# A two-layer decoder trunk: activations and norm weights laid out on the host, and another warm-up of TensorE

## The chip, the cores and the metric

The kernel runs on one core of one Trainium2 chip. The metric is the device time of one execution in microseconds (us); lower is better. TensorE (PE in the profile) multiplies, ScalarE (ACT) and VectorE (DVE) prepare its operands, GpSimd (POOL) does small things, and SyncE (SP) issues most of the loads. SP, ACT and POOL each have a DMA queue of their own; all queues share the core's 16 DMA engines.

## The reference, cut to what matters

Two layers work on 256 tokens of width 1024. What the change touches is the start of each layer, and the per-layer embedding `p`:

```python
h = x                                               # (256, 1024) float32
for i in range(DEPTH):                              # 2 layers
    f = swiglu(rms_norm(h, ffn1_pre_g[i]), ffn1_w_gu[i], ffn1_w_down[i])   # 1024 -> 2 x 2816 -> 1024
    h = h + 0.5 * rms_norm(f, ffn1_post_g[i])
    ...                                             # two attentions, merged by gates; a second SwiGLU
    gate = jax.nn.sigmoid(rms_norm(h, ple_pre_g[i]) @ w_ple_gate[i])
    e = (p[i] @ w_ple_proj[i]) * gate               # p[i]: (256, 256)
    h = h + rms_norm(e, ple_post_g[i])
```

All inputs are float32.

## The kernel before, in words

**Units and slots.** All weights are streamed once. They are cut into units of 1 MB (2048 columns on 128 partitions), numbered in the order in which TensorE uses them, and a unit lives in one of three slots (`SLOTS = 3`, unit number modulo 3) of three buffers: `raw` as loaded, `w_hi` and `w_lo` as split. Each product is made exact enough by three products of rounded parts: weight high x input high, weight low x input high, weight high x input low. So each unit is loaded by SP, its high part is rounded off by ACT (`high`, `high_piece`), its low part is subtracted by DVE (`low`, `low_piece`), and only then is it multiplied. The norm's weight vector (`ffn1_pre_g` and its like) is multiplied into the weights in these two steps (`scale=g_layer[...]`), so it must stand as a column over the partitions; the norm's root goes in behind the product, where the Silu reads it (`r_pre`). Products on TensorE wait for DVE's count `split_done` or `piece_split`.

**The head of the program.** Unit 0 is `w_ple_proj` (the product `p @ w_ple_proj` of layer 0 is made first and kept in `e_keep`); units 1 and 2 are the first 256 + 256 gate and up columns of layer 0's first SwiGLU (two halves of the 1024 input rows), unit 3 and unit 4 the next such columns, unit 5 the first rows of the down weights. Units 0 to 3 (`PIECED = 4`) are loaded, rounded and split in four pieces each, so that work can begin with the first quarter. Unit 3 uses unit 0's slot: SP issues its loads only when DVE has split all of unit 0. TensorE starts on unit 3 only when all four pieces are split (`begin`), and the second half of its columns only when the products of gate and up of units 1 and 2 are made for both token tiles (`prod_done`): that needs ACT's mean square of `h` (`square_pre`), POOL's root of it, ACT's Silu and DVE's product, for tile 0 and then for tile 1.

**ACT's order in the head** is written out by hand: pieces of units 0 to 2 between the inputs, two pieces of unit 3, `square_pre` of tile 0, the other two pieces of unit 3, the Silu of tile 0, `square_pre` of tile 1, half of unit 4, the Silu of tile 1, the other half of unit 4. Engines work through their instructions in this order; nothing overtakes.

**Turning.** TensorE needs the inputs with tokens last (input channels on the partitions), but `x` and `p` come with tokens on the partitions. So TensorE transposes them 128 x 128 at a time against an identity, into PSUM: `x` in four groups of four (`turn`), `p` in groups of two in layer 0 and one group of four in layer 1 (`turn_p`); ACT rounds the high part out of PSUM and DVE subtracts the low part. `x` is loaded into `h` (it is the residual too) in four loads of 256 KB on ACT's queue. The norm weights are loaded as rows by POOL and turned the same way in two steps (`turn_first_gain`, `turn_gains`). Until the first `p` is there, TensorE transposes the identity 13 and 3 times (`WARM_UP = (13, 3)`), so as not to stand idle.

Of the kernel before, what the change touches and what calls it, by code (L numbers as in the profile page):

```python
# [62 lines left out]
WARM_UP = (13, 3)  # L63
# [14 lines left out]
def trunk_kernel(nc, a, out):  # L78
    with ExitStack() as ctx:
# [34 lines left out]
        g_cols = sb("g_cols", [P, 4, (DEPTH + 1) * KD])  # L114
# [64 lines left out]
        p_nat = soft[:, :, 0:PLE]  # L179
# [9 lines left out]
        g_rows = mixed_t[:, P:2 * P]  # L189
# [21 lines left out]
        p_turned = sem("p_turned")  # L211
# [5 lines left out]
        h_loaded = [sem(f"h_loaded{n}") for n in range(2 * TT)]  # L217
# [56 lines left out]
        first_g = sem("first_g")  # L274
# [10 lines left out]
        p_in = [sem(f"p_in{t}") for t in range(TT)]  # L285
        first_g_in = sem("first_g_in")
# [5 lines left out]
        cols_turned = sem("cols_turned")  # L292
# [8 lines left out]
        blank = sem("blank")  # L301
        out_done = sem("out_done")
# [4 lines left out]
        HT_BANK, P_BANK, FIRST_P_BANK = 6, 7, (3, 5)  # L307
# [10 lines left out]
        GAIN_BANK = (4, 5)  # L318
# [48 lines left out]
        X_FIRST = (0, 2, 1, 3)  # L367
        X_FIRST_BANK = (0, 0, 1, 1)

        def p_bank(i, t=0):  # L370
            return bank(P_BANK if i else FIRST_P_BANK[t]).rearrange("p (k n) -> p k n", k=2)

        def nth_p(i, t):

            return i + 1 + (t if i == 0 else 1)

        def x_bank(i, q, idx):

            return bank((X_FIRST_BANK if (i, q) == (0, 0) else X_BANK[q])[idx])

        def nth_x(i, q, idx):

            return 20 * i + 4 * q + (X_FIRST.index(idx) if (i, q) == (0, 0) else idx) + 1

# [23 lines left out]
        def _(sp_):  # L408
            def load_p(t):
                sp_.dma_start(p_nat[:, t, :], a["p"][0, 0, t * P:(t + 1) * P, :]).then_inc(p_in[t], 16)  # L410

            for t in range(TT):
                load_p(t)
# [48 lines left out]
            for u in range(1, PIECED):  # L462
                load_pieces(u)
# [28 lines left out]
        def _(pool):  # L492
            pool.memset(ident[:, :], 0.0).then_inc(blank, 1)
# [3 lines left out]
            pool.dma_start(g_rows[0:2 * KD, :], a["ffn1_pre_g"].rearrange("l (k p) -> (l k) p", p=P)  # L497
                           ).then_inc(first_g_in, 16)
            for n, name in ((1, "mix_pre_g"), (2, "ffn2_pre_g"), (3, "ple_pre_g")):
                pool.dma_start(g_rows[2 * KD * n:2 * KD * (n + 1), :],  # L500
                               a[name].rearrange("l (k p) -> (l k) p", p=P)).then_inc(g_in, 16)
# [1615 lines left out]
```

## Time and profile before

| | us |
|---|---|
| three timed executions | 1174.38, 1173.87, 1173.72 |
| median | 1173.87 |
| span of the profiled execution, first to last instruction | 1172.6 |
| PE busy in it | 1164.0 |
| DVE busy | 850.0 |
| ACT busy | 721.0 |

The median stands 1.27 us above the profiled span. The page's first part gives each engine's busy time, and its fourth part follows the chain of waits back from the last instruction. For a change at the head of the program the views by stretch (busy time, DMA share and GB/s in a window), the timeline of one engine and the time from a DMA's issue to its landing say more than the averages.

### The profile page before, as it was taken

How to read it: one execution, taken by the hardware profiler on the slowest of the kernel's cores; microseconds unless marked ns; L12 is line 12 of the kernel's file. 1: busy time of each engine (PE TensorE's matmuls, PEld its weight loads, DVE VectorE, ACT ScalarE, POOL GpSimd, SP SyncE). 2: the span in 40 equal slices, each digit the busy share in tenths (PEclk: the TensorE clock that was granted, in tenths of full speed). 3: DMA queues.
4: the chain of work that ended last, by engine and by line, in shares of the span. 5: the costliest groups of instructions: out<-in, count | busy, mean ns of one | idle time of the engine just before them, and what ended most of it. 6: DMA issues, size and time to landing. Idle time of an engine off the chain costs nothing.

```text
span 1172.6 us, 17196 instructions
## 1 busy us (share of the span) xinstructions
PE 1164.0 (99%) x6031; PEld 983.8 (84%) x6031; DVE 850.0 (72%) x1290; ACT 721.0 (61%) x1166; POOL 53.0 (5%) x124
## 2 busy tenths in 40 slices
PE   9999999999999999999999999999999999999997
PEld 7888888888888888888888888888888888888886
DVE  6766776977857776676787776678776677677666
ACT  7555556577755755555685655565776566565555
POOL 4000000000000000000100000010000010000002
PEclk9999999999999999999999999999999999999999
DMA  9656564654354555655556565746434446546550
GB/s 296 217 181 212 171 215 164 226 172 152 121 201 146 191 204 185 208 174 211 179 171 198 172 211 179 240 165 198 171 111 179 162 162 215 194 170 209 179 196 37
DMA packets 138655, 215.37 MB, mean 184 GB/s; under 512 B 6958, under 2 KB 97904, under 8 KB 138608
## 3 DMA queue, kind: packets, MB, share of 16 engines
q1 hardware_dynamic: 135808, 208.43, 52.6%
q10 hardware_dynamic: 2576, 6.29, 1.6%
q8 instruction: 28, 0.46, 0.2%
q14 instruction: 19, 0.16, 0.0%
q0 software_dynamic: 224, 0.04, 0.0%
HBM read 213.68 MB, written 1.05 MB: 183 GB/s over the span
## 4 chain that ended last, share of the span: by engine, by line
PE 99%; DMA 0%; DVE 0%; ACT 0%; issue 0%; POOL 0%; POOLq 0%; DVEq 0%; ACTq 0%
PE ps L1673 23%; PE ps L1546 19%; PE ps L1548 18%; PE ps L1547 18%; PE ps L1683 12%; PE ps L1916 3%; PE ps L1593 1%; PE ps L1925 1%; PE ps L1802 1%; PE ps L1817 1%; PE ps L1776 0%; PE ps L1788 0%; DMA raw<-in_w_ple_proj 0%; PE ps L1831 0%; PE ps L1838 0%; PE ps L1803 0%
## 5 line engine op out<-in xcount | busy, mean ns | idle before, releaser
L1106 DVE SCALAR_TENSOR_TENSOR w_lo<-raw,g_layer,w_hi 128x512 fp32r<-128x512 f32 (+1 forms) x504 | 356.3, 767 | 139.2 <-ACT w_hi L644 139.2
L644 ACT ACTIVATE w_hi<-raw,g_layer 128x512 fp32r<-128x512 f32 (+1 forms) x524 | 346.7, 732 | 113.6 <-PE ps L1683 97.0
L1673 PE MATMUL ps<-x_both,w_hi 128*128 128x512 f32 x1152 | 287.7, 392 | 0.0
L1673 PEld LDWEIGHTS ps<-x_both,w_hi 128*128 128x128 f32 x1152 | 209.3, 189 | 39.4 <-issue 0.4
L1546 PE MATMUL ps<-w_hi,x_both 128*128 128x512 f32 x576 | 231.6, 402 | 0.0
L1548 PE MATMUL ps<-w_hi,x_both 128*128 128x512 f32 x576 | 225.0, 391 | 0.0
L1547 PE MATMUL ps<-w_lo,x_both 128*128 128x512 f32 x576 | 224.4, 390 | 0.0
L1103 DVE TENSOR_TENSOR w_lo<-raw,w_hi 128x1024 fp32r<-128x1024 f32 x114 | 134.8, 1221 | 61.3 <-ACT w_hi L641 61.3
L641 ACT ACTIVATE w_hi<-raw 128x1024 fp32r<-128x1024 f32 x114 | 114.7, 1053 | 92.7 <-PE ps L1548 92.5
L1683 PEld LDWEIGHTS ps<-x_both,w_lo 128*128 128x128 f32 x1152 | 152.6, 191 | 8.4
L1683 PE MATMUL ps<-x_both,w_lo 128*128 128x256 f32 x1152 | 156.0, 283 | 0.0
L1546 PEld LDWEIGHTS ps<-w_hi,x_both 128*128 128x128 f32 x576 | 108.2, 188 | 25.9 <-issue 3.0
L1548 PEld LDWEIGHTS ps<-w_hi,x_both 128*128 128x128 f32 x576 | 108.1, 188 | 23.4
L1547 PEld LDWEIGHTS ps<-w_lo,x_both 128*128 128x128 f32 x576 | 108.4, 188 | 19.9
L1546 PE MATMUL ps<-w_hi,ht_hi 128*128 128x512 f32 x320 | 124.9, 390 | 0.0
L1548 PE MATMUL ps<-w_hi,ht_lo 128*128 128x512 f32 x320 | 124.5, 389 | 0.0
L1547 PE MATMUL ps<-w_lo,ht_hi 128*128 128x512 f32 x320 | 124.5, 389 | 0.0
L726 ACT ACTIVATE glu<-glu 128x512 f32<-128x512 f32 x36 | 22.8, 633 | 78.5 <-DVE glu L1154 78.5
L1548 PEld LDWEIGHTS ps<-w_hi,ht_lo 128*128 128x128 f32 x320 | 60.1, 188 | 12.5
L1547 PEld LDWEIGHTS ps<-w_lo,ht_hi 128*128 128x128 f32 x320 | 60.1, 188 | 12.3
L1546 PEld LDWEIGHTS ps<-w_hi,ht_hi 128*128 128x128 f32 x320 | 60.1, 188 | 12.3
L1156 DVE TENSOR_TENSOR glu<-glu,prob 128x512 f32<-128x512 f32 x36 | 24.9, 693 | 27.6 <-ACT glu L726 27.6
(230 smaller groups left out, 1041.7 us busy)
## 6 DMA issues: line engine op xcount, KB each, us to landing
raw<-in_ffn_w_gu SPq DMA_DIRECT2D x170, 512.0 KB, 4.6
raw<-in_ffn_w_down SPq DMA_DIRECT2D x88, 512.0 KB, 4.0
raw<-in_w_in SPq DMA_DIRECT2D x80, 512.0 KB, 4.5
raw<-in_w_out SPq DMA_DIRECT2D x16, 512.0 KB, 4.1
raw<-in_w_ple_gate SPq DMA_DIRECT2D x16, 512.0 KB, 4.1
raw<-in_w_branch_sb SPq DMA_DIRECT2D x8, 512.0 KB, 4.1
raw<-in_w_branch_diff SPq DMA_DIRECT2D x8, 512.0 KB, 4.2
raw<-in_ffn_w_gu SPq DMA_DIRECT2D x12, 256.0 KB, 7.8
```

Source lines behind the costliest of these rows:

```text
L641: last = act.activation(w_hi[:, s, part], raw[:, s, part], ACT.Copy)
L644: last = act.activation(w_hi[:, s, part], raw[:, s, part], ACT.Copy, scale=g_layer[:, g:g + 1])
L726: act.activation(glu_g, glu_g, ACT.Silu).then_inc(silu_done, 2)
L1103: last = dve.tensor_tensor(w_lo[:, s, part], raw[:, s, part], whi[:, part], ALU.subtract)
L1106: last = dve.scalar_tensor_tensor(out=w_lo[:, s, part], in0=raw[:, s, part], scalar=g_layer[:, g:g + 1], in1=whi[:, part], op0=ALU.mult, o ...
L1156: dve.tensor_tensor(glu_g, glu_g, wide_r, ALU.mult).then_inc(silu_scaled, 1)
L1546: pe.matmul(dst, x_h, w_h, start=first, stop=False, **group)
L1547: pe.matmul(dst, x_h, w_l, start=False, stop=False, **group)
L1548: return pe.matmul(dst, x_l, w_h, start=False, stop=last, **group)
L1673: mm = pe.matmul(dst, w_hi[:, s, cols], x_both[:, :, 4 * half + k, :], start=half == 0 and k == 0, stop=stop and k == 3, skip_group_check= ...
L1683: mm = pe.matmul(bank(FLAT_BANK[j])[:, 0:SEQ], w_lo[:, s, cols], x_hi[:, 4 * half + k, :], start=False, stop=False, skip_group_check=True)
L1916: mm = pe.matmul(dst, w_hi[:, s, cols], x_both[:, :, 4 * half + k, :], start=half == 0 and k == 0, stop=stop and k == 3, skip_group_check= ...
```

## The change

The host now also hands over `x_t` (x transposed, 1024 x 256), `p_t` (p transposed per layer) and `gains` (all pre-norm weights and the sub-norm's as columns, 33 per layer). All transposes of `x` and `p` in layer 0, of `p` in layer 1, and of the norm weights go. `x_t` is loaded in four loads of 256 KB on ACT's queue into buffers that are idle then (`sbq_t`, `sbk_t`), `x` itself is still loaded into `h` as the residual, now by two 512 KB loads on SP's queue between units 2 and 3. `p`'s high part of layer 0 is rounded by DVE instead of ACT. The first product runs piece by piece with both tiles. TensorE's warm-up is four products of 256 columns on a buffer of ones (`squares`), which DVE fills first.

```diff
-WARM_UP = (13, 3)
+WARM_UP = 4
...
 # SP
-            for t in range(TT):
-                load_p(t)
+            for k in range(2):
+                sp_.dma_start(p_raw[:, k, :], a["p_t"][0, k * P:(k + 1) * P, :]).then_inc(p_in[k], 16)
...
             load_pieces(U_PROJ, (1, 3))
-            for u in range(1, PIECED):
-                load_pieces(u)
+            load_pieces(1)
+            load_pieces(2)
+            for t in range(TT):
+                sp_.dma_start(h[:, t, :], a["x"][0, t * P:(t + 1) * P, :]).then_inc(h_loaded[t], 16)
+            load_pieces(3)
...
 # POOL
+            pool.dma_start(g_all[:, :, :], a["gains"].rearrange("l p n -> p l n")).then_inc(g_in, 16)
...
 # ACT
+            def high_x(n):
+                act.wait_ge(x_in[n], 16)
+                act.activation(x_hi[:, 2 * n:2 * n + 2, :], x_raw[n], ACT.Copy).then_inc(x_high, 1)
...
             def square_pre(i, n, t):
                 act.wait_ge(h_ready, 16 * i + 4 * n + 2 * t + 2)
+                if (i, n) == (0, 0):
+                    act.wait_ge(h_loaded[t], 16)
...
-            high_piece(U_PROJ, 0)
-            high_p(0, 0, slice(0, P))
-            high_piece(U_PROJ, 2)
-            high_p(0, 1, slice(P, SEQ))
-            high_piece(U_PROJ, 1)
-            high_piece(U_PROJ, 3)
+            for k in (0, 2, 1, 3):
+                high_piece(U_PROJ, k)
             load_x(1)
-            high_inputs(0, 0, 0, (0,))
-            act.wait_ge(first_g, 1)
+            high_x(0)
+            act.wait_ge(layer_g, 1)
             high_piece(1, 0)
             high_piece(1, 1)
+            load_x(2)
+            high_x(1)
+            high_piece(1, 2)
+            high_piece(1, 3)
             load_x(3)
-            high_piece(1, 2)
-            high_inputs(0, 0, 1, (0,))
-            high_piece(1, 3)
+            high_x(2)
             high_piece(2, 0)
             for t in range(TT):
                 keep_e(0, t)
             high_piece(2, 1)
-            high_inputs(0, 0, 0, (1,))
+            high_x(3)
             high_piece(2, 2)
             high_piece(2, 3)
             high_piece(3, 0)
             high_piece(3, 1)
-            high_inputs(0, 0, 1, (1,))
             square_pre(0, 0, 0)
...
 # DVE
+            dve.memset(squares[:, :], 1.0).then_inc(blank_pe, 1)
...
 # PE
+            def warm_up():
+                pe.wait_ge(blank_pe, 1)
+                for _ in range(WARM_UP):
+                    mm = pe.matmul(bank(GU_BANK[0])[:, 0:SEQ], squares[:, 0:P], squares[:, :], start=True, stop=True)
+                mm.then_inc(units_used, SLOTS)
...
+            warm_up()
+            first_proj()
             pe.wait_ge(const_id, 1)
-            warm_up(WARM_UP[0])
-            turn_p(0, (0,))
-            warm_up(WARM_UP[1])
-            turn_p(0, (1,))
-            first_proj()
...
-                ffn(i, 1, 3, U_FFN2, (lambda: turn_p(i + 1)) if i < LAST else (lambda: None))
+                ffn(i, 1, 3, U_FFN2)
```

How the change moves instructions is shown at two places. The first is SP's queue, from its first load to unit 5. Rows give line, operation, destination and source, and shape; `in_ffn_w_gu` in `128x2x256` are pieces of units 1 to 3, in `128x4x256` the halves of unit 4. Before:

```order
L410 DMA soft<-in_p 128x256 x2
L446 DMA raw<-in_w_ple_proj 128x512 x2
L446 DMA raw<-in_ffn_w_gu 128x2x256 x12
L419 DMA raw<-in_ffn_w_gu 128x4x256 x2
L419 DMA raw<-in_ffn_w_down 128x1024 x2
```

and SP's queue now:

```order
L401 DMA soft<-in_p_t 128x256 x2
L434 DMA raw<-in_w_ple_proj 128x512 x2
L434 DMA raw<-in_ffn_w_gu 128x2x256 x8
L453 DMA h<-in_x 128x1024 x2
L434 DMA raw<-in_ffn_w_gu 128x2x256 x4
L407 DMA raw<-in_ffn_w_gu 128x4x256 x2
L407 DMA raw<-in_ffn_w_down 128x1024 x2
```

The two loads of `x` into `h` now stand in front of unit 3's four pieces and all that follows.

The second place is ACT from the end of unit 1 to unit 4; the last `L655` rows (now `L640`) are pieces of unit 3, `L644` (now `L629`) is unit 4, `L682` (now `L674`) is `square_pre`, `L739` (now `L731`) the Silu. Before:

```order
L655 ACTIVATE w_hi<-raw,g_layer 128x512 x2
L668 ACTIVATE e_keep<-ps 128x1024 x2
L655 ACTIVATE w_hi<-raw,g_layer 128x512
L675 ACTIVATE x_both<-ps 128x4x128
L655 ACTIVATE w_hi<-raw,g_layer 128x512 x4
L675 ACTIVATE x_both<-ps 128x4x128
L682 ACTIVATE tmp,mean_pre<-h 128x1024
L655 ACTIVATE w_hi<-raw,g_layer 128x512 x2
L739 ACTIVATE glu<-ps,r_pre 128x256
L682 ACTIVATE tmp,mean_pre<-h 128x1024
L644 ACTIVATE w_hi<-raw,g_layer 128x512 x2
```

and ACT now:

```order
L640 ACTIVATE w_hi<-raw,g_layer 128x512
L658 ACTIVATE e_keep<-ps 128x1024 x2
L640 ACTIVATE w_hi<-raw,g_layer 128x512
L646 ACTIVATE x_both<-sbk_t 128x512
L640 ACTIVATE w_hi<-raw,g_layer 128x512 x4
L674 ACTIVATE tmp,mean_pre<-h 128x1024
L640 ACTIVATE w_hi<-raw,g_layer 128x512 x2
L731 ACTIVATE glu<-ps,r_pre 128x256
L674 ACTIVATE tmp,mean_pre<-h 128x1024
L629 ACTIVATE w_hi<-raw,g_layer 128x512 x2
```

The rounding of the last quarter of `x` between the pieces of unit 3 and `square_pre` is gone; the order of the pieces, `square_pre`, Silu and unit 4 has stayed.

## Rows read from the trace of the kernel before

**Rows 1.** The page: span, busy times, and the chain's shares by engine.

```profile
span 1172.6 us, 17196 instructions
PE 1164.0 (99%) x6031; PEld 983.8 (84%) x6031; DVE 850.0 (72%) x1290; ACT 721.0 (61%) x1166; POOL 53.0 (5%) x124
...
PE 99%; DMA 0%; DVE 0%; ACT 0%; issue 0%; POOL 0%; POOLq 0%; DVEq 0%; ACTq 0%
```

**Rows 2.** Busy time by stretch; the last columns are granted clock, DMA share, GB/s.

```profile
3.00:6.00 3.00, 3.00 (x15) 2.71 (x13) 0.90 (x2) 2.52 (x4) 3.00 (x15) 1.00 1.05 392
...
18.00:21.00 3.00, 3.00 (x17) 2.50 (x16) 2.50 (x4) 2.91 (x5) 0.00 (x0) 1.00 1.10 347
22.00:23.00 1.00, 1.00 (x6) 0.81 (x5) 1.00 (x2) 1.00 (x3) 0.23 (x1) 1.00 1.04 389
30.00:60.00 30.00, 30.00 (x163) 26.01 (x162) 23.17 (x32) 16.94 (x29) 0.00 (x0) 1.00 0.63 211
```

**Rows 3.** Timeline, SP's issues: start, time on the queue, line, load, count.

```profile
2.66 10.22 SPq L446 DMA_DIRECT2D raw<-in_ffn_w_gu  x12
...
15.71 0.94 SPq L419 DMA_DIRECT2D raw<-in_ffn_w_gu  x2
```

**Rows 4.** DMA issues at 12.27 us and at 16.14 us: KB, us to landing.

```profile
raw<-in_ffn_w_gu SPq DMA_DIRECT2D x1, 256.0 KB, 8.2
...
raw<-in_ffn_w_gu SPq DMA_DIRECT2D x1, 512.0 KB, 7.1
```

**Rows 5.** Timeline of ACT and DVE: the first piece, and unit 2 to unit 4.

```profile
4.44 0.63 ACT L655 ACTIVATE w_hi<-raw 128x512 fp32r<-128x512 f32 x1 [0.46 <-DMA raw<-in_w_ple_proj]
...
18.36 2.55 ACT L655 ACTIVATE w_hi<-raw,g_layer 128x512 fp32r<-128x512 f32 x4
...
21.55 1.05 ACT L682 ACTIVATE tmp<-h 128x1024 f32<-128x1024 f32 x1
...
22.59 1.33 ACT L655 ACTIVATE w_hi<-raw,g_layer 128x512 fp32r<-128x512 f32 x2
...
23.34 1.41 DVE L1087 SCALAR_TENSOR_TENSOR w_lo<-raw,g_layer,w_hi 128x512 fp32r<-128x512 f32 x2 [0.30 <-ACT w_hi L655]
...
23.82 0.46 ACT L739 ACTIVATE glu<-ps,r_pre 128x256 f32<-128x256 f32 x1
...
24.17 1.06 ACT L682 ACTIVATE tmp<-h 128x1024 f32<-128x1024 f32 x1
...
25.21 1.33 ACT L644 ACTIVATE w_hi<-raw,g_layer 128x512 fp32r<-128x512 f32 x2
...
27.91 0.48 DVE L1171 SCALAR_TENSOR_TENSOR glu<-ps,r_pre,glu 128x256 f32<-128x256 f32 x1
```

**Rows 6.** Timeline of PE: start of work, and unit 3.

```profile
1.59 3.04 PE L2008 MATMUL ps<-ident 128*128 128x128 f32 x13 [1.59 <-POOL ident L495]
...
6.77 0.63 PE L1547 MATMUL ps<-w_lo,p_hi 128*128 128x512 f32 x1
...
7.20 0.46 PE L1548 MATMUL ps<-w_hi,p_lo 128*128 128x512 f32 x1
...
25.67 1.98 PE L1673 MATMUL ps<-x_both,w_hi 128*128 128x512 f32 x8
...
28.44 2.14 PE L1673 MATMUL ps<-x_both,w_hi 128*128 128x512 f32 x8
```

**Rows 7.** Timeline of PE around the transposes of p in layer 1.

```profile
550.46 0.39 PE L1547 MATMUL ps<-w_lo,x_both 128*128 128x512 f32 x1
550.69 0.39 PE L1548 MATMUL ps<-w_hi,x_both 128*128 128x512 f32 x1
550.92 0.60 PE L2001 MATMUL ps<-ident,soft 128*128 128x128 f32 x4
...
551.59 0.40 PE L1547 MATMUL ps<-w_lo,ht_hi 128*128 128x512 f32 x1
```

**Rows 8.** Busy time by stretch behind the last product, as rows 2.

```profile
1165.70:1167.80 2.10, 0.00 (x0) 0.00 (x0) 1.64 (x5) 1.52 (x4) 0.90 (x3) 1.00 0.67 250
1167.90:1172.60 4.70, 0.00 (x0) 0.00 (x0) 1.80 (x3) 0.00 (x0) 0.81 (x1) 0.50 0.30 112
```

## What I predict, and from what

> **What bounds the kernel now.** I read the page first: PE is busy for 1164.0 of the 1172.6 us of the span, and 99% of the chain that ended last is PE [rows 1]. So the time is PE's own work from its first useful product to its last, and only two things can change it: work taken off PE, and a wait on PE. The next view is busy time by stretch [rows 2]. In the body (30 to 60 us) the DMA engines are busy for 0.63 of the time and move 211 GB/s, so loads have room there. In the head it is another picture: from 3 us on the DMA share stands at 1.05 to 1.10, and the engines move 392 GB/s at first and still 347 between 18 and 21 us. SP has issued all pieces of units 1 to 3 by 12.9 us [rows 3], and the last of them, issued at 12.27, lands 8.2 us later, at 20.5; the second half of unit 4, issued at about 16.14, lands 7.1 us later, at 23.2 [rows 4]. The loads stand in a full queue, so what is put ahead of them moves them back. The third view is the timeline around unit 3 [rows 5, 6]: ACT rounds its last two pieces from 22.59 on, DVE ends their low parts at 24.75 (23.34 + 1.41), PE takes the unit up at 25.67; ACT begins unit 4 at 25.21, DVE's product of tile 1 ends at 28.39 (27.91 + 0.48), and PE starts the second half of unit 3 at 28.44, 0.05 us behind it. There DVE's product, behind ACT's chain, is what PE meets last. In the before kernel all of this just fits.
>
> **Work taken off PE in layer 1.** One group of four transposes of `p` goes. From 550.69 to 551.59 two products and the group take 0.90 us; two products alone take 2 x 0.23 (550.46 to 550.69), so the group costs 0.90 - 0.45 = 0.45 us [rows 7]. PE is the bound there and nothing hides it: a gain of 0.45 us. ACT now rounds `p` out of a loaded buffer and DVE subtracts the same 512 columns as before, both at the same place in their order; the load was there before too. I cost these at nothing, with the body's DMA room and PE's bound as the cover.
>
> **Work taken off PE in the head.** Four groups of `x` go (4 x 0.45 = 1.8 us), and the three transposes of norm weights. The first product can start when ACT has the first high piece, at 4.44 + 0.63 = 5.07 [rows 5], since `p`'s high part no longer goes through PSUM. Units 0 to 2 are 72 products of 0.227 us, 16.3 us: PE would be done with unit 2 at 21.4 if it never waited. It does wait for pieces. ACT's pieces of unit 2 end in before at 18.36 + 2 x 0.64 = 19.6 (a row of four spans units 2 and 3 [rows 5]); the norm weights now come without PE, and ACT no longer waits for transposes, so I put that about 0.9 us earlier, at 18.8. DVE's low part of 0.75 follows, and PE still has the last piece of tile 0 and twelve products of tile 1 to do (3 x 0.23 + 12 x 0.23 = 3.4): end of unit 2 at about 23.0 to 23.3, against 25.6 in before. So PE gains about 2.3 us by the end of unit 2, with bounds of 0 and 4.2.
>
> **The warm-up** has no row of its own: no product of ones stands in before. Its bounds: if the clock is at its upper level from the first useful product, that saves what the first products lost (the second, at 6.77, took 0.43 to the next start at 7.20 against 0.23 later [rows 6]; with the first some 0.6 us in all). If it rises as late after PE's first work as in before, 5.7 us (1.59 to about 7.3), or some us later, PE is up to 2 us later at the end of unit 2. (The granted clock of these stretches reads 1.00 [rows 2]; the durations show the lower level.) Both ends fall into a wait that I come to now, so I take nothing for it.
>
> **What the change adds: 1 MB of loads in the head.** Before, `x` was loaded once and served both as residual and for the transposes. Now `x_t` is loaded where `x` was, and `x` again, ahead of unit 3 in SP's queue. The engines are full there, so 1.05 MB costs its own time: at 389 GB/s, which a stretch full of long runs showed (22 to 23 us [rows 2]), 2.7 us; at 347, 3.0 us. `x_t` comes in runs of 1 KB instead of 2 KB, at worst 0.3 us more. I take 2.8; bounds 2.4 (if the head's first microseconds, with fewer small loads of norm weights, give some back) and 3.3.
>
> **What is late by that.** Unit 3's last piece lands at 20.5 + 2.8 = 23.3, the ones before it 0.75 us apart (256 KB at 350 GB/s): 22.55, 21.8 for the second. ACT stands idle before them, since it has ended unit 2 at 18.8. Its second piece of unit 3 starts at 21.8; a piece takes 0.62 to the next start, so `square_pre` of tile 0 starts at 22.4, and 1.04 later (21.55 to 22.59 [rows 5]) the third piece, 23.45; the fourth 24.1. In before these were 22.59 and 23.2. ACT's fourth piece ends at 24.8, DVE's low part at 25.55, and PE starts unit 3 at 25.6: the same time as before. The 2.3 us that PE had gained are spent waiting, with some 2.4 us of idle PE. Then the Silu of tile 0 follows the fourth piece (0.6 behind its start: 24.7), `square_pre` of tile 1 at 25.05, unit 4 at 26.1; unit 4 has landed by 23.2 + 2.8 = 26.0. Before, ACT began unit 4 at 25.21: 0.9 earlier. The same chain of ACT and DVE hangs on it (half of unit 4, Silu of tile 1, product), so PE's second half of unit 3 starts at 28.44 + 0.9 = 29.35 instead of 28.44. PE meets it with 0.95 us of idle time, as its first half takes 2.77 (25.67 to 28.44). Behind this place PE's work is as before, 0.9 us later; with 0.63 of the DMA engines busy the loads catch up, and I see no further wait. The span is 1172.6 + 0.9 - 0.45 = 1173.05; the median stood 1.27 above the span, so the forecast is **1174.3 us**.
>
> **Rival A, the second load of `x` costs nothing.** If unit 3 lands by about 20.9, as in before (the loads of the head packed better than the shares say, or ACT's gaps filled), PE goes from unit 2 into unit 3 at 23.3 and gains 2.3 + 0.45 = 2.75: 1171.1. Against it: a DMA share over 1.05 in every stretch of the head [rows 2] and 8.2 us to landing [rows 4]. For it: only that I read queue order from issue order. It decides from a landing of unit 3's second piece before about 20 us; each microsecond between is worth about one microsecond.
>
> **Rival B, the wait costs the clock.** Behind the last product PE's clock went from 1.00 to 0.50 at about 1167.9, within 2.3 us after PE's last product ended, before 1165.7 [rows 8]. The wait for unit 3 would be about 2.4 us long. If the clock falls to 1.2 GHz in it, unit 3 runs at half speed until it rises, which took 5.7 us at the start: PE loses 5.7 / 2 = 2.85, less the 0.95 of idle time that the slower work fills, so 1.9 later than the forecast: 1176.2, slower than before by 2.3. It decides from a wait of about 2 us. For it: rows 8. Against: only one of the two waits is that long. The Trainium skill, page TensorE: Matmul & The Clock Gate, section Why this matters for your kernels, advises against long idle gaps between bursts of products because the clock then drops; rows 8 agree that it drops, no row here shows a gap amid products; by that rule the time would be this rival's, 1176.2.
>
> **Rival C, the load is dearer.** With 3.3 us for the extra load and a late end of unit 4 the chain is 0.5 to 1.5 us later: 1174.8 to 1175.8. And if the new warm-up does not keep PE awake, so that the first products run at half speed for longer, the loss of up to 2 us falls into the same wait: the time of the forecast.
>
> **How the numbers follow.** A measurement of this kernel tells a change of about 0.2%, 2.35 us, from none: faster is below 1171.5, slower above 1176.2. The forecast (with rival C's near end) has 0.62, its own range 1173.0 to 1175.5; A 0.14, between 1170.6 and 1172.5; B 0.18, between 1175.2 and 1177.5; C's far end 0.06. Faster: most of A, 0.12. Slower: about two thirds of B and half of C's far end, 0.16. Same: 0.72. The range leaves out the fast half of A and the slow part of B: 1171.6 to 1176.7.
>
> **What would show it.** In the changed kernel's timeline: the first product at about 5.1; unit 2 done on PE by 23.3; SP's load of unit 3's last piece landing at about 23.3; PE idle for over 2 us before unit 3, with DVE's low part of unit 3 as the releaser, and unit 3 starting near 25.6; the second half near 29.35; no transposes of `p` in layer 1. The forecast is wrong if PE goes into unit 3 without a wait (A), if the products of unit 3 take twice their 0.23 us (B), or if a later stretch of PE shows waits that before did not have.

## The result, and the profile after

The change makes the kernel slower. The changed kernel took 1179.55 us (median of 5; 1179.00 to 1179.64), the kernel before beside it 1174.18 (median of 5): ratio 1.0046, interval 1.0034 to 1.0058. That is 5.4 us more, and it lies above the predicted range, which ended at 1176.7. The profiled execution took 1179.55 us with a span of 1177.8, 5.2 longer than the span before.

The page answers [rows 1]: span, busy time, and the chain that ended last.

```profile
span 1177.8 us, 17121 instructions
PE 1163.3 (99%) x5996; PEld 980.7 (83%) x5996; DVE 850.3 (72%) x1291; ACT 720.4 (61%) x1164; POOL 50.6 (4%) x120
...
PE 98%; DMA 1%; DVE 0%; ACT 0%; issue 0%; POOL 0%; SPq 0%; POOLq 0%; DVEq 0%; ACTq 0%
```

TensorE (PE) is busy 0.7 us less and the span is 5.2 us longer, so PE waits more. A DMA has come into the chain with 1% where PE alone stood. The view by stretch (PE's busy time first; the last three columns are PE's granted clock, the share of DMA time, GB/s) shows where, in answer to [rows 2]:

```profile
12.00:15.00 3.00, 1.62 (x6) 1.05 (x6) 0.78 (x2) 0.00 (x0) 2.49 (x7) 1.00 1.08 384
15.00:18.00 3.00, 0.00 (x0) 0.00 (x0) 0.62 (x2) 1.28 (x3) 0.77 (x3) 1.00 1.05 390
18.00:21.00 3.00, 2.11 (x5) 1.75 (x6) 2.31 (x5) 2.14 (x4) 0.00 (x0) 0.62 1.07 334
21.00:24.00 3.00, 3.00 (x12) 2.37 (x12) 1.32 (x3) 3.00 (x5) 0.00 (x0) 0.82 1.02 316
```

PE does nothing from 15 to 18 us. Behind the gap the granted clock is 0.62 and 0.82: part of these stretches runs at 1.2 GHz. The timeline of PE (start, time, line, operation; in brackets the idle time before it and what ended it) has the places themselves, in answer to [rows 6]:

```profile
1.25 3.78 PE L1987 MATMUL ps<-squares 128*128 128x256 f32 x8 [1.25 <-DVE squares L1029]
5.20 0.70 PE L2000 MATMUL ps<-w_hi,p_hi 128*128 128x512 f32 x2 [0.17 <-ACT w_hi L640]
...
13.49 0.39 PE L1539 MATMUL ps<-w_hi,x_both 128*128 128x512 f32 x1
18.89 0.76 PE L1537 MATMUL ps<-w_hi,x_both 128*128 128x512 f32 x1 [5.01 <-DVE w_lo L1066]
19.45 0.63 PE L1538 MATMUL ps<-w_lo,x_both 128*128 128x512 f32 x1
...
22.30 0.39 PE L1539 MATMUL ps<-w_hi,x_both 128*128 128x512 f32 x1
...
30.03 1.98 PE L1662 MATMUL ps<-x_both,w_hi 128*128 128x512 f32 x8
...
32.88 1.43 PE L1662 MATMUL ps<-x_both,w_hi 128*128 128x512 f32 x5
```

The wait lies in the middle of unit 1, between 13.72 (13.49 + 0.23) and 18.89: 5.2 us. The eight products that start from 18.89 to 22.01 take 3.41 us instead of 8 x 0.23 = 1.84: 1.6 us go to the clock. PE begins unit 3 at 30.03 without any wait; in the kernel before it did at 25.67, its second half at 28.44 [rows 6]. So the head has put PE 4.4 us back. The view of waits between 5 and 31 us follows it to its origin (who waited, for what: us in total, times, longest):

```profile
PEld ps L1537 <- DVE x_both L1429: 5.4, 1, 5.4
DVE x_both L1429 <- ACT x_both L646: 5.3, 2, 4.6
ACT x_both L646 <- DMA sbq_t<-in_x_t: 4.8, 1, 4.8
```

PE waits for DVE's low part of the input, DVE for ACT's high part, ACT for the second quarter of the transposed `x`. ACT's timeline and the view of DMA issues at 8.9 us (KB, us from issue to landing) tell of that load:

```profile
8.92 0.38 ACTq L607 DMA_DIRECT2D sbq_t<-in_x_t  x1
...
16.72 0.63 ACT L646 ACTIVATE x_both<-sbq_t 128x512 fp32r<-128x512 f32 x1 [4.77 <-DMA sbq_t<-in_x_t]
...
23.52 2.56 ACT L640 ACTIVATE w_hi<-raw,g_layer 128x512 fp32r<-128x512 f32 x4
```

```profile
h<-in_x SPq DMA_DIRECT2D x1, 512.0 KB, 9.0
sbq_t<-in_x_t ACTq DMA_DIRECT2D x1, 256.0 KB, 7.8
```

ACT issues the second quarter only when it has rounded the pieces of unit 0, at 8.92 us, and it lands 7.8 us later. SP has by then issued all eight pieces of units 1 and 2. All that ACT does next stands behind that load; the last two pieces of unit 2, the first half of the row of four, come at 23.52. The kernel before also issued its third and fourth load of `x` at about 9 and 11 us, but its first two loads held the first 512 channels of both token tiles, all that unit 1 needs; now the first load holds 256 channels of both, half of unit 1.

In layer 1 the four transposes of `p` are gone. PE's timeline at the place of [rows 7]:

```profile
555.45 0.39 PE L1538 MATMUL ps<-w_lo,x_both 128*128 128x512 f32 x1
...
556.13 0.39 PE L1538 MATMUL ps<-w_lo,ht_hi 128*128 128x512 f32 x1
```

From the first to the last of these products pass 0.68 us, with two more between them; for the same products [rows 7] have 1.13 (550.46 to 551.59). The difference is 0.45 us.

The rest is in no single row. For the same product in both traces I took how much later it starts than in the kernel before (us; at unit 3 and its second half a product just behind the first, whose own start is stretched by a wait; each row is one profiled execution; below the changed kernel stand kernels of the experiments):

| | unit 3 | its second half | 320 us | 352 us | 548 us | 552 us | 905 us | 925 us | end |
|---|---|---|---|---|---|---|---|---|---|
| changed kernel | 4.36 | 4.43 | 4.54 | 4.93 | 4.99 | 4.53 | 4.66 | 5.00 | 5.15 |
| e4_x_in_order | 0.06 | 0.97 | 1.10 | 1.49 | 1.54 | 1.08 | 1.11 | 1.45 | 1.53 |
| e6_in_order_padded | 0.35 | 1.24 | 1.19 | 1.19 | 1.23 | 0.77 | 0.70 | 0.70 | 0.70 |
| e13_silu_ahead | 0.92 | 0.83 | 0.79 | 0.79 | 0.84 | 0.38 | 0.34 | 0.34 | 0.38 |

So 5.15 = 4.43 (head) + 0.56 (to 548 us) - 0.46 (transposes of `p`) + 0.62 (from 552 to the end). The 1.2 us lost in the body was in no part of the prediction.

### The profile page after: what moved, and what is told of

Read it like the earlier page. It is cut to its first block, busy times and chain, and to the rows that moved or that the text cites. A ratio compares the mean times of both kernels' runs of the same rounds, so it can differ in the third digit from the quotient of the medians.

```text
span 1177.8 us, 17121 instructions
## 1 busy us (share of the span) xinstructions
PE 1163.3 (99%) x5996; PEld 980.7 (83%) x5996; DVE 850.3 (72%) x1291; ACT 720.4 (61%) x1164; POOL 50.6 (4%) x120
## 4 chain that ended last, share of the span: by engine, by line
PE 98%; DMA 1%; DVE 0%; ACT 0%; issue 0%; POOL 0%; SPq 0%; POOLq 0%; DVEq 0%; ACTq 0%
PE ps L1662 22%; PE ps L1537 18%; PE ps L1539 18%; PE ps L1538 18%; PE ps L1672 12%; PE ps L1902 2%; PE ps L1582 1%; PE ps L1911 1%; DMA sbq_t<-in_x_t 1%; PE ps L1788 1%; DMA raw<-in_w_ple_proj 1%; PE ps L1803 1%; PE ps L1762 0%; PE ps L1774 0%; PE ps L1817 0%; PE ps L1824 0%
## 5 line engine op out<-in xcount | busy, mean ns | idle before, releaser
L629 ACT ACTIVATE w_hi<-raw,g_layer 128x512 fp32r<-128x512 f32 (+1 forms) x524 | 346.7, 732 | 113.7 <-PE ps L1672 97.0
L718 ACT ACTIVATE glu<-glu 128x512 f32<-128x512 f32 x36 | 22.8, 633 | 78.5 <-DVE glu L1133 78.5
```

What stands on the lines that cost most here:

```text
L629: last = act.activation(w_hi[:, s, part], raw[:, s, part], ACT.Copy, scale=g_layer[:, g:g + 1])
L718: act.activation(glu_g, glu_g, ACT.Silu).then_inc(silu_done, 2)
```

## The experiments

### Theory L: the quarters of x are issued too late

Theory L: with full queues a load lands some 8 us after its issue, whatever its own size, so the three quarters of `x` that ACT issues between its rounding steps come late. Rival M: it is the extra megabyte of `x` for the residual. Theory C: much of the 5.4 us is the clock.

**One quarter earlier.** The second quarter is issued at the head, behind the first:

```diff
             load_x(0)
+            load_x(1)
             act.preload_act_table_set("silu_and_others")
...
-            load_x(1)
             high_x(0)
```

> One edit on the changed kernel: the second 256 KB load of x_t is issued at the head of ACT's program, right behind the first, instead of behind the rounding of unit 0 (8.92 us). Theory L (the second quarter of x_t, issued behind a full queue, arrives late, stalls PE by 5.2 us in unit 1 and costs the clock): it lands at about 10 us, the wait of PE from 13.7 to 18.9 us goes, the clock does not fall there. The third quarter, still issued late, would now be the next to hold PE, in unit 2, by 2 to 3 us: 1175 to 1177 us. Rival M (the second copy of x, 1 MB ahead of unit 3, costs the time, wherever PE waits): total bytes ahead of unit 3 are the same, so 1179 to 1180 us.

Measured: 1180.46 us (1179.97 to 1181.15). The wait in the middle of unit 1 shrank to 0.3 us, as L says, but the time did not fall; it lies above both ranges, M's too. The next quarter was late instead, by the same mechanism: issued at 11.8 us, landed 8.2 us later. Its PE timeline at unit 2, and the stretches behind it:

```profile
22.19 0.77 PE L1537 MATMUL ps<-w_hi,x_both 128*128 128x512 f32 x1 [3.10 <-DVE w_lo L1066]
```

```profile
21.00:24.00 3.00, 1.62 (x3) 0.83 (x3) 1.32 (x3) 3.00 (x5) 0.00 (x0) 0.53 1.08 341
24.00:27.00 3.00, 2.47 (x6) 1.78 (x7) 3.00 (x6) 3.00 (x6) 0.00 (x0) 0.50 0.22 75
```

The wait is shorter, but the clock stayed at its lower level from 21 to 27 us and more. My expectation missed since I freed one load and left two in the same place.

**The residual's loads behind unit 3's pieces.**

```diff
-            for t in range(TT):
-                sp_.dma_start(h[:, t, :], a["x"][...]).then_inc(h_loaded[t], 16)
             load_pieces(3)
+            for t in range(TT):
+                sp_.dma_start(h[:, t, :], a["x"][...]).then_inc(h_loaded[t], 16)
```

> One edit on the changed kernel: SP issues the two loads of x into h behind the four pieces of unit 3 instead of ahead of them. Rival M: the pieces of unit 3 land 2.7 us earlier and the kernel with them, about 1176.8 us. Theory L: PE is held by the second quarter of x_t, which hardly moves, and unit 3 is not what PE waits for: 1178.5 to 1179.7 us.

Measured: 1179.16 us (1178.81 to 1179.32), 0.4 less than the changed kernel, as L expected. M falls as the cause of the 5.4 us.

**The quarters in the order of use.** The three later quarters go on SP's queue, each just ahead of the weight pieces that it is multiplied with:

```diff
-            load_pieces(1)
-            load_pieces(2)
+            load_pieces(1, (0, 1))
+            load_x(1)
+            load_pieces(1, (2, 3))
+            load_x(2)
+            load_pieces(2, (0, 1))
+            load_x(3)
+            load_pieces(2, (2, 3))
```

> On the changed kernel: the second to fourth quarters of x_t are issued by SP, each just ahead of the two pieces of weights that it is multiplied with, instead of by ACT as it comes to them. Theory L: each quarter lands with its weights, PE has no wait of over 1 us in units 1 and 2 and no fall of the clock there; what is left is the wait for unit 3 that the prediction priced: 1173 to 1175.5 us. Rival M: the bytes ahead of unit 3 are the same, 1179 to 1180 us.

Measured: 1175.51 us (1175.00 to 1176.20; ratio 1.0012, interval 1.0002 to 1.0022): 4.0 of the 5.4 us are gone, and L stands. With that load mended the head is the one of the prediction. Its PE timeline, and its waits from 18 to 31 us:

```profile
25.65 2.08 PE L1668 MATMUL ps<-x_both,w_hi 128*128 128x512 f32 x8 [1.77 <-DVE w_lo L1072]
...
29.43 0.96 PE L1668 MATMUL ps<-x_both,w_hi 128*128 128x512 f32 x3 [0.75 <-DVE glu L1156]
```

Unit 2's last product ends its turn at 23.72, unit 3 begins at 25.65 and its second half at 29.43; the prediction had 23.0 to 23.3, 25.6 and 29.35.

**All quarters at the head.** Is it the time of issue, or that ACT's queue comes second to SP's? ACT issues all four loads in its first 4 us:

```diff
             load_x(0)
+            load_x(1)
+            load_x(2)
+            load_x(3)
```

> The changed kernel with all four quarters of the transposed x issued by ScalarE's queue at the head, in its first 4 us, instead of one at a time behind the rounding of weights. Theory L (a load lands as long after its issue as bytes stand ahead of it; the quarters of the changed kernel came late because they were issued late): all four land by about 12 us, the pieces of unit 1 up to 2.3 us later than they did, TensorE starts unit 1 between 12 and 14 us, has no wait of 5 us in it, and the granted clock does not fall; the time is 1175.2 to 1176.7 us. Rival O (ScalarE's queue is served behind SP's as long as SP's has loads, whatever the time of issue): the third and fourth quarter land after 17 us again and the time is 1178 us or more.

Measured: 1175.42 us (1175.26 to 1175.99). L's number. The view of DMA issues from 1.5 to 4.5 us:

```profile
sbq_t<-in_x_t ACTq DMA_DIRECT2D x2, 256.0 KB, 7.7
sbk_t<-in_x_t ACTq DMA_DIRECT2D x2, 256.0 KB, 9.5
```

The same queue, issued early, has all quarters in by 13.2 us, and the granted clock reads 1.00 from 12 to 24 us. Rival O falls: what counts is when a load is issued and how many bytes stand ahead of it.

### What the clock costs

**Products on ones in the wait.** At the place of the wait 22 products on ones (later 10) keep PE at work:

```diff
                 def wait():
+                    if (u, k) == (U_FFN1, 2):
+                        for _ in range(22):
+                            pe.matmul(bank(0)[:, 0:SEQ], squares[:, 0:P], squares[:, :], start=True, stop=True)
```

> One edit on the changed kernel: before PE's wait for the second quarter of x_t (unit 1, third piece) PE makes 22 products of 256 columns on ones into an idle PSUM bank, about 4.7 us of them at full clock, inside the wait of 5.2 us. Theory L with a price for the clock: the wait stays, the clock holds at 1.00 through 18 to 22 us, and the eight products that ran at 0.43 us apart run at 0.23: 1.4 to 1.7 us less, 1177.7 to 1178.2 us. If the fall of the clock were hidden behind another wait: 1179 to 1180 us.

Measured: 1181.84 us (1181.78 to 1181.99). The clock stayed at 1.00 from 12 to 24 us, but the block was mis-sized. Its row on PE's timeline:

```profile
13.78 9.66 PE L1641 MATMUL ps<-squares 128*128 128x256 f32 x44
```

One such product in this type stands as two rows, so 22 took 9.3 us and overran the wait by 4: unit 1 went on at 23.09 instead of 18.89. With ten:

> The changed kernel with ten products on ones (256 columns, two rows of 0.216 us each, so 4.3 us) at the place in unit 1 where TensorE waits for the second quarter of the transposed x from 13.7 to 18.9 us; they fit into that wait, as the earlier try with 22 of them did not. Theory C (the clock's fall behind that wait costs 1.6 us of the 5.4): the granted clock stays at 1.00 and the time is 1177.9 us (1177.7 to 1178.4). Rival D (the time behind the wait is set by the next quarters and unit 3's pieces, so that a faster clock only waits for them): the clock stays up too, but the time is 1179.0 us or above, the same as the changed kernel within 0.5 us.

Measured: 1179.20 us (1178.51 to 1179.77), rival D's number; the profiled execution is the fastest of the five and lies between C and D. The block ran from 13.31 to 17.8 us and PE went straight on. The clock read 1.00, and PE reached unit 3 0.9 to 1.4 us earlier than in the changed kernel (shift 2.92 at unit 3, 3.52 at its second half, against 4.36 and 4.43). On the way it met new waits, in its view of waits from 17 to 33 us:

```profile
PE ps L1537 <- DVE w_lo L1066: 0.6, 2, 0.4
PE ps L1665 <- DVE glu L1150: 0.5, 1, 0.5
```

So the clock's fall costs 1.6 us where it happens. Without it the profiled execution ends about 1 us earlier, and the medians differ by 0.35 us, which lies within their spread: as D said, most of what the clock gives back is spent waiting for what comes next. Most of the 5.4 us is the wait itself.

### The megabyte behind unit 3

In e4_x_in_order PE still met the 0.9 us at unit 3's second half that the prediction had put down to the extra megabyte.

**Both: quarters in order, the residual behind unit 3's pieces** (the two edits above together):

> The version with quarters 2 to 4 of the transposed x on SP's queue just ahead of the weight pieces that are used with them took 1175.5 us; TensorE stood 0.97 us behind the kernel before from unit 3 on. This run moves in addition the two loads of x into h (1 MB) from ahead of unit 3's pieces to behind them, the one edit against that version. Theory M (the extra megabyte ahead of unit 3 is what holds TensorE there): the bytes ahead of unit 3 are again those of the kernel before, the 0.97 us go to between 0 and 0.3, the second half of unit 3 starts at 28.4 to 28.8 us instead of 29.43, and the time is 1174.6 us (1174.4 to 1174.9). Rival Q (the places of x among the pieces hold it, not the extra bytes): no change, 1175.5 us. Rival S (the square of h, which then waits for a later h, becomes the late one): h lands after 24 us, the root mean square reaches unit 1's first use later, and the time is above 1176 us.

Measured: 1175.87 us (1175.18 to 1176.29). Unit 3 began earlier, at 25.20, but its second half at 29.31, still 0.86 late. The time is near Q's, but the places of `x` among the pieces are not what the rows show. ACT's timeline has two waits:

```profile
21.84 1.06 ACT L683 ACTIVATE tmp<-h 128x1024 f32<-128x1024 f32 x1 [1.92 <-DMA h<-in_x]
...
26.08 1.34 ACT L638 ACTIVATE w_hi<-raw,g_layer 128x512 fp32r<-128x512 f32 x2 [0.46 <-DMA raw<-in_ffn_w_gu]
27.32 0.46 ACT L740 ACTIVATE glu<-ps,r_pre 128x256 f32<-128x256 f32 x1
```

The first is rival S's, for a later `h`, shorter than S expected. The second is for unit 4's load, until 26.08, and the Silu of tile 1, whose product PE waits for, is queued behind that. The megabyte is ahead of unit 4 in both orders.

**Squares early.** A version of e4_x_in_order with the tensors at their old addresses (below) in which ACT squares both tiles of `h` ahead of unit 3's pieces:

```diff
+            square_pre(0, 0, 0)
+            square_pre(0, 0, 1)
-            high_piece(3, 0)
-            high_piece(3, 1)
-            square_pre(0, 0, 0)
-            high_piece(3, 2)
-            high_piece(3, 3)
+            for k in range(4):
+                high_piece(3, k)
             first_silu(0, 0, U_FFN1)
-            square_pre(0, 0, 1)
```

> The version with x in order and the tensors back at their addresses (1175.2 us), with one edit: ScalarE squares both tiles of h ahead of unit 3's pieces, where it stands idle for 1.85 us waiting for the first of them, instead of between and behind them. Theory U (what is late in the head is ScalarE's chain of unit 3's pieces, two squares, Silu and unit 4): unit 3's last piece is rounded by 24.0 instead of 24.7, TensorE starts unit 3 at 24.6 to 25.2, the Silu of the second tile runs ahead of 26 us, the wait of 0.9 us at the second half of unit 3 goes, and from there TensorE is 0.3 to 1.0 us ahead of the kernel before instead of 1.2 behind it; with the 0.45 us of layer 1 the time is 1172.6 to 1173.6 us, below both kernels. Rival N (unit 4's load, which lands at 26.1, holds the Silu that is queued behind its rounding, so the second half of unit 3 starts as late as now): 1174.9 to 1175.3 us.

Measured: 1174.93 us (1174.13 to 1175.31), rival N's number. PE began unit 3 at 25.76, later than U asked. ACT is now done with unit 3's pieces at 24.7 and with the Silu of tile 0 at 25.0, and then idle until unit 4 lands:

```profile
26.74 1.34 ACT L638 ACTIVATE w_hi<-raw,g_layer 128x512 fp32r<-128x512 f32 x2 [1.70 <-DMA raw<-in_ffn_w_gu]
27.98 0.45 ACT L740 ACTIVATE glu<-ps,r_pre 128x256 f32<-128x256 f32 x1
```

**The Silu ahead of unit 4**, in addition, and DVE's product likewise, in this place alone:

```diff
-                high(i, u0 + 3, g0 + 4, halves=(0,))
+                if (i, f) != (0, 0):
+                    high(i, u0 + 3, g0 + 4, halves=(0,))
                 act.wait_ge(pre_scale, 8 * i + 4 * f + 2)
                 silu(i, f, 0, u0 + 1, 1)
+                if (i, f) == (0, 0):
+                    high(i, u0 + 3, g0 + 4, halves=(0,))
```

> The version with x in order, the tensors at their old addresses and both squares early (1174.9 us), with one edit: for unit 3 ScalarE runs the Silu of the second tile ahead of rounding the first half of unit 4, and VectorE its product ahead of that half's low part. In that version the Silu started at 27.98 us behind the rounding that waited for unit 4's load until 26.74, TensorE waited for the product and was 0.17 us behind the kernel before at unit 3 and 1.52 at its second half. Theory Z (what the extra megabyte costs behind unit 3 is the Silu queued behind unit 4's load): that wait of 1.3 us goes, the shift stays near 0.2 us through layer 0 and ends near -0.3; 1173.7 us (1173.4 to 1174.1). Rival K (unit 4's weights themselves are then late for TensorE): TensorE waits behind unit 3 instead, and the time is 1174.7 us or above.

Measured: 1173.66 us (1173.05 to 1174.73), Z's number; the kernel before beside it took 1174.19 (ratio 0.9995, interval 0.9986 to 1.0004). Both Silus now stand together, ahead of the wait for unit 4, and PE's second half of unit 3 follows without a wait:

```profile
25.40 0.82 ACT L740 ACTIVATE glu<-ps,r_pre 128x256 f32<-128x256 f32 x2
27.69 2.56 ACT L638 ACTIVATE w_hi<-raw,g_layer 128x512 fp32r<-128x512 f32 x4 [1.47 <-DMA raw<-in_ffn_w_gu]
```

```profile
26.51 2.08 PE L1672 MATMUL ps<-x_both,w_hi 128*128 128x512 f32 x8 [1.28 <-DVE w_lo L1073]
29.38 2.00 PE L1672 MATMUL ps<-x_both,w_hi 128*128 128x512 f32 x8
```

The profiled execution is the slowest of its eleven (1174.73): there unit 3's pieces landed late and PE began it at 26.51, 0.8 to 0.9 us behind the kernel before. What the row shows is that the second half adds nothing to that. The median is 0.5 us below that of the kernel before beside it, which is within the interval: at best the change is worth nothing that can be told from no change.

**All mended terms together**: all quarters at the head, old addresses, squares early, Silu ahead.

> The version with all quarters of the transposed x issued at the head (1175.4 us; TensorE 0.11 us ahead of the kernel before at unit 3, 0.53 behind at its second half) with the same three edits: old addresses, squares early, Silu and product of the second tile ahead of unit 4's first half. If theory Z holds and all terms add (0.65 us of wait behind unit 3, 1.0 us of addresses), the shift stays near -0.1 through layer 0 and ends near -0.6: 1173.4 us (1173.1 to 1173.8), below the kernel before. If K holds: 1174.4 us or above.

Measured: 1174.86 us (1174.18 to 1177.39); missed. The terms do not add. The number is K's, but not by K's mechanism: PE goes from the first half of unit 3 into the second without a wait. In the profiled execution PE waited 2.0 us for the first weight piece of unit 1, which stands behind all of `x`, twice more within unit 1 (0.6 and 0.4 us), and the clock fell in it:

```profile
13.74 0.47 PE L1541 MATMUL ps<-w_hi,x_both 128*128 128x512 f32 x1 [1.88 <-DVE w_lo L1067]
...
15.68 0.63 PE L1542 MATMUL ps<-w_lo,x_both 128*128 128x512 f32 x1
```

```profile
15.00:18.00 3.00, 2.91 (x7) 2.00 (x8) 3.00 (x6) 2.97 (x5) 2.64 (x5) 0.51 1.06 386
```

In e12_x_all_at_head the first nine products of unit 0 ran at the lower clock, and PE came to unit 1 later, with less to wait. The clock is not all of the miss: six of the eleven executions read a mean granted clock of 0.999, as most of the kernel before do, and took 1174.2 to 1175.2 us. What the rest is stays open.

### The 1.2 us in the body

More than half of it (0.62 us) sits in the 96 products on `os_hi` and `os_lo`, 48 a layer; the view of that tensor gives their durations (ns: least, median, most). In the kernel before, in the changed kernel:

```profile
L1547 PE MATMUL ps<-w_lo,os_hi x32: 389/389/395, 331.0 to 921.5; 128*128 128x512 f32 x32
```

```profile
L1538 PE MATMUL ps<-w_lo,os_hi x32: 394/399/403, 335.6 to 926.5; 128*128 128x512 f32 x32
```

The same operation with the same shapes is 10 ns longer; from start to start the medians are 232 to 237 ns instead of 227. The change replaced `g_cols` (384 bytes a partition) by `g_all` (264, for which 288 are set aside), and all tensors behind it moved down by 96 bytes: `os_hi` began at a multiple of 64 bytes (208768) and now begins 32 bytes into one (208672).

**Back to the old addresses**, on e4_x_in_order:

```diff
-        g_all = sb("g_all", [P, DEPTH, 33])
+        g_all = sb("g_all", [P, DEPTH, 48])
...
-            pool.dma_start(g_all[:, :, :], ...
+            pool.dma_start(g_all[:, :, 0:33], ...
```

> Against the version with x in order on SP's queue (1175.5 us) one edit: the tensor g_all gets 48 columns a layer instead of 33, of which 33 are used, so that every on-chip tensor behind it lies at the byte address that it had in the kernel before (384 bytes a partition instead of 264; the tensors behind it, os_hi and os_lo among them, had moved down by 96 bytes). In all versions of the changed kernel TensorE loses about 0.5 us a layer against the kernel before, two thirds of it in the 96 products on os_hi and os_lo, whose distance is 232 to 237 ns instead of 227. Theory A (the addresses do it): the distance is 227 ns again, the shift to the kernel before stays at 0.97 us from unit 3 to the end of layer 0 and ends at 0.5 us, and the time is 1174.5 us (1174.3 to 1174.8). Rival B (something else of the change does it, such as which loads and engines run beside them): the distance stays at 232 to 237 ns and the time at 1175.5 us.

```profile
L1544 PE MATMUL ps<-w_lo,os_hi x32: 389/389/395, 332.2 to 922.2; 128*128 128x512 f32 x32
```

Measured: 389 ns again, and no drift: the table above has 1.24, 1.19, 1.23 in layer 0 and 0.77 to 0.70 in layer 1, where e4_x_in_order went from 0.97 to 1.54 and from 1.08 to 1.53. The time, 1175.22 us (1174.45 to 1176.32), missed A's range: it is 0.3 below e4_x_in_order instead of 1.0. The profiled execution began unit 3 0.3 later than that of e4_x_in_order; that the medians differ from the forecast for the same reason is not shown.

**The kernel before, moved by 32 bytes**, with nothing of the change in it:

```diff
         g_cols = sb("g_cols", [P, 4, (DEPTH + 1) * KD])
+        shift = sb("shift", [P, 8])
```

> The kernel before with one edit: an unused tensor of 32 bytes a partition behind the gains, which moves every on-chip tensor behind it by 32 bytes, so that os_hi and os_lo start 32 bytes into a block of 64 as they do in the changed kernel. Nothing else of the change is in it. Theory A (the addresses cost the 1 us that the changed kernel loses outside its head): the products on os_hi and os_lo are 232 to 237 ns apart instead of 227, and the time is 1174.7 to 1175.1 us. Rival B (not the addresses): 1174.1 us and 227 ns.

```profile
L1548 PE MATMUL ps<-w_lo,os_hi x32: 392/396/396, 330.8 to 922.0; 128*128 128x512 f32 x32
```

Measured: 1175.09 us (1174.69 to 1175.76) beside 1174.06 for the kernel before: 1.0 us for 32 bytes (ratio 1.0009, interval 1.0000 to 1.0018). In the profiled execution the product goes from 0.4 us ahead of the kernel before at unit 3 to 0.5 behind it at the end. Both ways round, the address is the cause.

### The warm-up

**One product on ones instead of four**, on e4_x_in_order: `WARM_UP = 1`.

> The version with x in order on SP's queue (1175.5 us), with one product on ones at the start instead of four. The prediction took nothing for the warm-up, since what TensorE loses in its first products falls into waits that follow. Theory W: the first products of the projection of p run at the lower clock, 0.43 us apart, and the clock record rises some us later than 5.0 us, but the idle time between 7.5 and 13.9 us (0.5, 0.8 and 0.5 us) and the 1.9 us ahead of unit 3 take that in; the time is 1175.5 us within 0.4. Rival V (the clock stays low so long that unit 1 and 2 run late by more than the 4 us of idle time that follow): 1177 us or more.

Measured: 1175.62 us (1175.23 to 1176.86), against 1175.51 with four. PE's timeline has the products at 1.2 GHz until 10 us:

```profile
4.84 1.19 PE L2006 MATMUL ps<-w_hi,p_hi 128*128 128x512 f32 x2 [2.31 <-ACT w_hi L649]
...
10.10 0.70 PE L2006 MATMUL ps<-w_hi,p_hi 128*128 128x512 f32 x2
```

Twelve products, from 4.84 to 10.10 us, lose 0.2 us each, 2.4 us, and all of it falls into waits that were there anyway: PE begins unit 3 at 25.25, no later than e4_x_in_order. W holds.

## Why the prediction was wrong

**The step that failed** stands in the part on the head: "ACT no longer waits for transposes, so I put that about 0.9 us earlier, at 18.8", and from it "end of unit 2 at about 23.0 to 23.3". It took the arrival of `x` for granted. Measured, ACT waited 4.8 us for the second quarter and ended unit 2's pieces near 24.8 (23.52 + 2 x 0.64) instead of 18.8, and PE ended unit 2 at 30.0. The prediction knew that a load issued at 12.27 lands 8.2 us later [rows 4]; it applied that to units 3 and 4 and not to the quarters of `x`, which ACT issues from 8.92 on. Nor did it see that the first load covers half of unit 1 where the first two before covered all. With the measured wait put in, its sum comes out: 23.2 + 5.2 (wait) + 1.6 (clock) = 30.0, and unit 3 began at 30.03. That it comes out so closely is in part luck: the 23.2 held a wait for unit 2's last pieces, which PE did not meet; it met 1.4 us of others, at the third piece of unit 0 and ahead of unit 1. e4_x_in_order and e12_x_all_at_head, which issue the same bytes earlier, give 4 us back.

**The wait for unit 3 and the 0.9 us behind it** were right in mechanism and size as soon as the quarters came in time (25.65 and 29.43 against 25.6 and 29.35). In the changed kernel itself PE came so late that it met neither. The landing behind them was there: the last two pieces of unit 3 took 10.5 us (median), and the last, issued at 12.2, landed at 22.8, against 23.3 in the forecast and 20.5 before. The view of DMA issues from 12 to 14 us:

```profile
raw<-in_ffn_w_gu SPq DMA_DIRECT2D x2, 256.0 KB, 10.5
```

The chain named (unit 4's load, then the Silu of tile 1 in ACT's order, then DVE's product) is the one that e13_silu_ahead cut.

**The warm-up** was rightly put at nothing. The first product came at 5.20 (forecast 5.1) at the upper clock, and a warm-up cut to one product cost nothing that the medians tell (1175.62 against 1175.51).

**Layer 1** gave the 0.45 us, in every version of the changed kernel.

**Rival A** (the second load costs nothing) did not come: unit 3's last piece landed 2.3 us later than before, and e4_x_in_order has PE waiting 1.9 us ahead of unit 3.

**Rival B** (the wait costs the clock) was right that a gap amid products lowers the clock, and wrong in place and price. In unit 3, where it expected the fall, a wait of 1.9 us left the clock at 1.00 in e4_x_in_order; in unit 1, where no wait was foreseen, it fell and took 1.6 us on the spot, of which products in the gap gave 0.35 back in the medians, within their spread. In e14_all_at_head_silu a wait of 2.0 us with one of 0.6 close behind it did bring it down. The Trainium skill, page TensorE: Matmul & The Clock Gate, section Why this matters for your kernels, warns of this, and here a trace shows it amid products.

**Rival C** gave up to 1175.8 for a dearer load. The second load of `x` was not dearer: unit 3's last piece landed 2.3 us later, where the forecast took 2.8. What held PE was another load, a quarter of `x_t` that came late, with everything queued behind it.

**What no step held** is the 1.2 us in the body. The prediction said "Behind this place PE's work is as before" and had no term for a tensor of another size. A term for addresses was missing; e6_in_order_padded and e7_before_shifted are its measure, 1.0 us.

**The frame** was off by 0.5 us: the prediction set 1.27 us between span and time, from the median; the profiled execution of the changed kernel has 1.75, and so have the others on record within 0.1. So the span of 1172.6 belongs to the slowest of the three executions (1174.38), not to the median. In all, against a forecast span of 1173.05: 3.5 us more in the head (4.43 instead of 0.9) and 1.2 in the body make 1177.8.

## What to carry to other kernels

When loads stand in a full queue, list for every load that the change issues or moves when it is issued, what was issued before it on any queue, and when its first reader needs it; a load issued in good time by the program's order can still be a queue's length late, and mending one of several such loads only shows the next. An in-order engine that waits for a load holds everything behind it, so work whose data are there goes ahead of the wait. When an on-chip tensor changes its size, look at the addresses of all tensors behind it, and compare the duration of one and the same product before and after.

## What the runs showed of the hardware that I had not expected

**A load issued on an idle queue did not start for 3 us.** ACT's second quarter was issued at 8.92 us, when ACT's queue (q10) had only the last packets of the first quarter left, which landed at 9.1. Between 9.2 and 12.0 us only SP's queue (q1) moved bytes, but for one packet of POOL's; from 12 to 14 us ACT's did too. The view of DMA queues (packets, MB, share of 16 engines) in these two stretches of the changed kernel:

```profile
q1 hardware_dynamic: 1035, 1.00, 109.6%
q0 software_dynamic: 1, 0.00, 0.0%
```

```profile
q1 hardware_dynamic: 488, 0.61, 90.2%
q10 hardware_dynamic: 128, 0.13, 19.4%
```

The Trainium skill, page DMA: Bandwidth & Descriptors, section Queues, rings and completion order, has each engine take turns between the queues that have work for it. By that rule the quarter would have moved at once beside SP's pieces, and 256 KB at half of 357 GB/s (the rate from 9.2 to 12 us) would have landed before 11 us, an estimate; it landed at 16.7. Here the order was nearly that of issue across both queues: SP's first load of `h`, issued 0.2 us before it, took 9.0 us. In the kernel before it was much the same: from 8.9 to 11 us one packet of ACT's queue moved, with two loads issued there, which took 6.1 us (median) beside 7.6 for SP's. Where in between the load stood, no view shows.

**32 bytes of address cost a product 2 to 4%**: from start to start 232 to 237 ns instead of 227, where `os_hi` and `os_lo` begin 32 bytes into a block of 64; the weight loads between them kept their 188 ns.

**A product of 256 columns on ones in fp32 takes two rows**, from start to start 0.43 us each at the lower clock (eight rows in 3.78 us) and 0.22 at the upper (44 rows in 9.66 us).
